# One fused transformer and state-space kernel: state-space steps by TensorE products, conditioning loads in four buffers, read-out of four rotation products

## The reference

```python
cond = jax.nn.silu(c)
for i in range(DEPTH):
    mod = cond @ ada_w[i] + ada_b[i]          # ada_w[i]: 1024 x 6144
    sh_m, sc_m, g_m, sh_f, sc_f, g_f = ...
    h = rms_norm_2(x, norm_mix[i]) * (1.0 + sc_m) + sh_m
...
def s5_mixer(h, ...):                          # 64 groups of 16 channels, 64 complex states each
    bu = einsum(u, bb)                         # complex drive of each state
    x_re, x_im = associative_scan(x[t] = ab * x[t-1] + bu[t])
    y = einsum(x_re, c_re) - einsum(x_im, c_im) + d_skip * u
    g = gelu(y);  ga, gb = split(g @ w_glu);  return ga * sigmoid(gb)
```

## Time and profile before

| what | value |
|---|---|
| median of three runs | 1781.01 us |
| profiled execution, its own time | 1783.83 us |
| its span, first to last instruction | 1782.1 us (1.7 us lie around it) |
| busy: TensorE, VectorE, ScalarE, GpSimd | 1691.1 us (95%), 797.1 (45%), 298.2 (17%), 58.8 (3%) |
| mean granted clock of TensorE | 0.975 of full speed |
| HBM read | 286.67 MB, 161 GB/s over the span |
| DMA issues | 440 weight slots and 96 conditioning blocks of 512 KB, 32 copies of H of 32 KB |

### The profile page before, as it was taken

One profiled execution on the slowest core, in us unless ns is written; L12 is line 12 of the kernel. 1 busy time (PEld: TensorE's weight loads), 2 busy tenths in 40 slices (PEclk: granted clock), 3 DMA queues, 4 the chain that ended last, 5 costly groups with the idle time before them and its releaser, 6 DMA issues.

```text
span 1782.1 us, 21562 instructions
## 1 busy us (share of the span) xinstructions
PE 1691.1 (95%) x8586; PEld 1428.3 (80%) x8586; DVE 797.1 (45%) x1732; ACT 298.2 (17%) x660; POOL 58.8 (3%) x84
## 2 busy tenths in 40 slices
PE   7989989999989999999999999999999778999998
PEld 6648878888878877888888785788888667888887
DVE  6644454341156413644345575456541274343310
ACT  2112210000024102100000322322220011122200
POOL 0000000000000000092000000000000000000000
PEclk9999999999999999999999999999999877999999
DMA  6333448865644563666554232244435302444445
GB/s 222 125 135 119 165 157 306 306 246 186 210 159 146 209 233 136 237 218 243 186 165 154 83 118 95 82 137 152 152 129 166 117 15 72 142 154 152 150 160 177
DMA packets 82900, 290.19 MB, mean 163 GB/s; under 512 B 13296, under 2 KB 13296, under 8 KB 82032
## 3 DMA queue, kind: packets, MB, share of 16 engines
q1 hardware_dynamic: 82800, 288.81, 47.8%
HBM read 286.67 MB, written 1.05 MB: 161 GB/s over the span
## 4 chain that ended last, share of the span: by engine, by line
PE 88%; DVE 8%; issue 1%; DMA 1%; ACT 1%; SPq 1%; DVEq 0%; ACTq 0%
PE acc L381 69%; PE acc L454 5%; PE acc L908 3%; PE acc L436 3%; PE acc L391 1%; PE score L582 1%; PE acc L558 1%; PE turned L593 1%; PE score L538 1%; DVE H L1383 1%; DVE rstd L1319 1%; PE acc L606 1%; SPq L348 1%; DMA ring<-stream 0%; DMA cols<-cols_in 0%
## 5 line engine op out<-in xcount | busy, mean ns | idle before, releaser
L381 PE MATMUL acc<-H,ring 128*128 128x256 f32 x3528 | 777.6, 382 | 21.7 <-DMA ring<-stream 9.9
L381 PEld LDWEIGHTS acc<-H,ring 128*128 128x128 f32 x3528 | 671.5, 191 | 126.0 <-issue 12.2
L381 PE MATMUL acc<-FFN,ring 128*128 128x256 f32 x1408 | 306.5, 381 | 0.0
L381 PEld LDWEIGHTS acc<-FFN,ring 128*128 128x128 f32 x1408 | 268.5, 191 | 37.2 <-issue 0.4
L381 PE MATMUL acc<-big,ring 128*128 128x256 f32 x880 | 192.1, 379 | 0.9 <-PE acc L381 0.9
L381 PEld LDWEIGHTS acc<-big,ring 128*128 128x128 f32 x880 | 166.9, 190 | 24.6 <-issue 2.0
L1538 DVE SCALAR_TENSOR_TENSOR bT<-bT,cond 128x1024 f32<-128x1024 f32 x84 | 109.0, 1298 | 68.1 <-DMA bT<-ada_in 61.0
L1735 DVE SCALAR_TENSOR_TENSOR pair<-acc,cols,pair 128x255 f32<-128x255 f32 x84 | 40.5, 482 | 121.5 <-ACT pair L1077 118.2
L1401 DVE TENSOR_TENSOR X<-acc,X 128x256 f32<-128x256 f32 x48 | 20.4, 425 | 156.1 <-PE acc L381 146.9
L1698 DVE TENSOR_TENSOR FFN<-pair,acc 128x256 f32<-128x256 f32 x42 | 17.7, 421 | 143.0 <-PE acc L381 142.1
L1403 DVE SCALAR_TENSOR_TENSOR X<-acc,mod,X 128x256 f32<-128x256 f32 x24 | 11.6, 484 | 147.9 <-PE acc L381 144.4
(11 more groups left out here) (407 smaller groups left out, 1327.4 us busy)
## 6 DMA issues: line engine op xcount, KB each, us to landing
ring<-stream SPq DMA_DIRECT2D x440, 512.0 KB, 3.3
bT<-ada_in SPq DMA_DIRECT2D x96, 512.0 KB, 4.4
big<-ssm_in SPq DMA_DIRECT2D x2, 1024.0 KB, 5.7
cols<-cols_in SPq DMA_DIRECT2D x1, 1169.5 KB, 7.2
X<-x_in SPq DMA_DIRECT2D x1, 1024.0 KB, 4.8
MEM<-mem_in SPq DMA_DIRECT2D x1, 1024.0 KB, 12.1
FFN<-H SPq DMA_DIRECT2D x32, 32.0 KB, 1.9
y_out<-X SPq DMA_DIRECT2D x1, 1024.0 KB, 3.9
```

What stands on the lines that cost most here:

```text
L381: mm = nc.tensor.matmul(dst, w[:, k * cols_per:(k + 1) * cols_per], r, start=first and n == 0, stop=last and n == len(src) - 1)
```

## The change

It does three things.

1. Conditioning blocks 0 to 53 go through four buffers (two in `bT`, two in `K`) in place of two; the others through the two in `bT` as before. The queue's wait before a block is on the last block that used the same buffer. In `up0` four blocks are issued after slots 0 to 3, none after 4 to 7, one after each of 8 to 31, and then eight; in `od_xb` the four blocks are issued after slots 0, 1, 6 and 7 (before: 0, 2, 4, 6), and used after tiles 2, 3, 6, 7 (before: 2, 3, 4, 5).
2. The norm of the state-space stage is one VectorE instruction a tile (into FFN), and ScalarE adds the shift and reorders the tokens (`shifted`). The copy of H is no longer made by 32 DMAs: TensorE picks the 32 channels by products with columns of the identity (`select`: 16 products with 128x32 weights and 64 columns a tile), and ScalarE copies the bank to FFN (`moved`).
3. VectorE's step has 8 instructions in place of 12: the rotation of the drive is two products of 512 columns, the two scans are one of 512 columns, and the rotation back is left as four products (one instruction of 512 columns and two of 256) whose sums `read_out` makes with twice the products (64 a tile, 128 records). `decays` fills 504 columns in place of 252; a memset gets smaller.

```diff
-    ("up0", list(range(28)) + list(range(28, 44, 2))), ("down0", range(0, 24, 4)), ("od_xb", range(0, 8, 2)),
+    ("up0", [0, 1, 2, 3] + list(range(8, 32)) + [32, 34, 36, 38, 40, 41, 42, 43]), ("down0", range(0, 24, 4)),
+    ("od_xb", (0, 1, 6, 7)),
+N_WIDE = 54
+ADA_HOME = [a % (4 if a < N_WIDE else 2) for a in range(N_ADA)]
+ADA_FREE = [max((b + 1 for b in range(a) if ADA_HOME[b] == ADA_HOME[a]), default=0) for a in range(N_ADA)]
-        ada_ring = [bT[:, i * SLOT:(i + 1) * SLOT] for i in range(2)]
+        ada_ring = [bT[:, i * SLOT:(i + 1) * SLOT] for i in range(2)] + [K[:, i * SLOT:(i + 1) * SLOT] for i in range(2)]
 # SyncE
-                    if ada >= 2:
-                        sp.wait_ge(ada_used, ada - 1)
+                    if ADA_FREE[ada]:
+                        sp.wait_ge(ada_used, ADA_FREE[ada])
-                if s == SLOT0["glu"] + RING - 1:
-                    for half in (1, 0):
-                        sp.wait_ge(norm_out, S5_NORMED + (2 if half else 4))
...
 # TensorE
+            def select(n):
+                i = S5_ORDER[n]
+                pe.wait_ge(s5_shifted, n + 1)
+                if n >= 2:
+                    pe.wait_ge(s5_moved, n - 1)
+                for jj in range(4):
+                    for j in range(CHUNK):
+                        mm = nc.tensor.matmul(turned[n % 2][32 * j:32 * j + 32, jj * CHUNKS:(jj + 1) * CHUNKS],
+                                              ident[:, 32 * jj:32 * jj + 32],
+                                              H[:, i * S + j * CHUNKS:i * S + (j + 1) * CHUNKS], start=True, stop=True)
+                mm.then_inc(s5_selected, 1)
-                    for part in range(2):
+                    for part, term in ((0, 0), (1, 1), (1, 2), (0, 3)):
-            for n in range(4):
-                local(n)
+            select(0)
+            select(1)
+            local(0)
             driven(0)
+            select(2)
             driven(1)
+            select(3)
+            local(1)
+            select(4)
+            select(5)
+            local(2)
+            select(6)
+            select(7)
+            local(3)
 # ScalarE
+            def shifted(n):
+                i = S5_ORDER[n]
+                act.wait_ge(s5_gained, n + 1)
+                nc.scalar.activation(at(H, i).rearrange("p (j c) -> p j c", j=CHUNK),
+                                     at(FFN, 16 + i).rearrange("p (c j) -> p j c", j=CHUNK), ACT.Identity,
+                                     bias=mod[:, 48 + i:48 + i + 1]).then_inc(s5_shifted, 1)
+            def moved(n):
+                i = S5_ORDER[n]
+                act.wait_ge(s5_selected, n + 1)
+                nc.scalar.activation(at(FFN, i), turned[n % 2][:, 0:S], ACT.Copy).then_inc(s5_moved, 1)
+            shifted(0)
+            for n in range(1, KD):
+                shifted(n)
+                moved(n - 1)
+            moved(KD - 1)
 # VectorE
-                if 2 <= k < 6:
+                if k in (2, 3, 6, 7):
                     ada(1)
-            scaled(X, KD, rstd[:], lambda k: mod_gain(1, 0, k), H, shift=lambda k: mod_col(1, 0, k), by_chunk=True)
+            for n, i in enumerate(S5_ORDER):
+                v.scalar_tensor_tensor(at(FFN, 16 + i), at(X, i), mod_gain(1, 0, i), rstd[:], ALU.mult, ALU.mult)\
+                    .then_inc(s5_gained, 1)
-                own(v.tensor_tensor(by_tile(a), by_tile(bank[:, :]), rot, ALU.mult))
-                own(v.tensor_tensor(b[:, re], bank[:, im], cos_i, ALU.mult))
-                own(v.tensor_tensor(b[:, im], bank[:, re], sin_i, ALU.mult))
+                own(v.tensor_tensor(by_tile(a), by_tile(bank), cos2, ALU.mult))
+                own(v.tensor_tensor(by_tile(b), by_tile(bank), sin2, ALU.mult))
                 dve.sem_inc(s5_driven, 1)
-                own(v.tensor_tensor(z[:, re], a[:, re], a[:, im], ALU.add))
-                own(v.tensor_tensor(z[:, im], b[:, re], b[:, im], ALU.subtract))
+                own(v.tensor_tensor(z[:, re], a[:, re], b[:, im], ALU.add))
+                own(v.tensor_tensor(z[:, im], a[:, im], b[:, re], ALU.subtract))
                 dve.wait_ge(s5_decays, n + 1)
-                own(v.tensor_tensor_scan(w[:, re], d, z[:, re], 0.0, ALU.mult, ALU.add))
-                own(v.tensor_tensor_scan(w[:, im], d, z[:, im], 0.0, ALU.mult, ALU.add))
-                own(v.tensor_tensor(by_tile(a), by_tile(w), rot, ALU.mult))
-                own(v.tensor_tensor(b[:, re], w[:, re], sin_i, ALU.mult))
-                own(v.tensor_tensor(b[:, im], w[:, im], cos_i, ALU.mult))
+                own(v.tensor_tensor_scan(w, d, z, 0.0, ALU.mult, ALU.add))
+                if n == 0:
+                    dve.wait_ge(s5_shifted, KD)
                 if n >= 2:
                     dve.wait_ge(s5_y, n - 1)
-                own(v.tensor_tensor(x[:, re], a[:, re], a[:, im], ALU.subtract))
-                own(v.scalar_tensor_tensor(x[:, im], b[:, re], -1.0, b[:, im], ALU.mult, ALU.subtract))
+                own(v.tensor_tensor(x[:, re], w[:, re], cos_i, ALU.mult))
+                own(v.scalar_tensor_tensor(x[:, im], w[:, im], -1.0, cos_i, ALU.mult, ALU.mult))
+                own(v.scalar_tensor_tensor(by_tile(x[:, 2 * S:4 * S]), by_tile(w), -1.0, sin2, ALU.mult, ALU.mult))
                 dve.sem_inc(s5_state, 1)
```

More of the change, by code:

```diff
@@ L66 @@
 assert N_ADA == 96 and ADA_AFTER == sorted(ADA_AFTER)
+N_WIDE = 54
+ADA_HOME = [a % (4 if a < N_WIDE else 2) for a in range(N_ADA)]
+ADA_TURN = [ADA_HOME[:a].count(ADA_HOME[a]) + 1 for a in range(N_ADA)]
+ADA_FREE = [max((b + 1 for b in range(a) if ADA_HOME[b] == ADA_HOME[a]), default=0) for a in range(N_ADA)]
 PARTS0, _n = {}, 0
@@ L242, in build_program @@
         mod_done = sem("mod_done")
-        ada_loaded = [sem(f"ada_loaded{i}") for i in range(2)]
+        ada_loaded = [sem(f"ada_loaded{i}") for i in range(4)]
         ada_used = sem("ada_used")
@@ L270, in build_program @@
         s5_kernels_out = sem("s5_kernels_out")
-        s5_moved = [sem(f"s5_moved{i}") for i in range(2)]
+        s5_gained = sem("s5_gained")
+        s5_shifted = sem("s5_shifted")
+        s5_selected = sem("s5_selected")
+        s5_moved = sem("s5_moved")
         s5_driven = sem("s5_driven")
@@ L340, in _ @@
                     sp.dma_start(V, ssm_in[1]).then_inc(c_in, 16)
-                if s == SLOT0["glu"] + RING - 1:
-                    for half in (1, 0):
-                        sp.wait_ge(norm_out, S5_NORMED + (2 if half else 4))
-                        for jj in range(4):
-                            for j in range(CHUNK):
-                                dst = FFN[32 * j:32 * j + 32, half * 1024:half * 1024 + 1024]
-                                src = H[32 * jj:32 * jj + 32, half * 1024:half * 1024 + 1024]
-                                sp.dma_start(dst.rearrange("p (i q c) -> p i q c", q=4, c=CHUNKS)[:, :, jj, :],
-                                             src.rearrange("p (i q c) -> p i q c", q=CHUNK, c=CHUNKS)[:, :, j, :])\
-                                    .then_inc(s5_moved[half], 16)
             sp.wait_ge(acc_free, 4 + TILE0["down3"] + 8)
@@ L846, in _ @@
             down("down2")
-            assert outs[0] == S5_NORMED
             sums(KD - 1)
-            outs[0] += 4
             def local(n):
                 i, t = S5_ORDER[n], TILE0["s5"] + n
-                pe.wait_ge(norm_out, S5_NORMED + 1 + n // 2)
+                pe.wait_ge(s5_shifted, n + 1)
                 bank_free(t)
@@ L887, in read_out @@
                                                   x[:, lo:lo + CHUNKS - 1], start=False,
-                                                  stop=l == CHUNK - 1 and part == 1)
+                                                  stop=l == CHUNK - 1 and term == 3)
                 mm.then_inc(s5_y, 1)
             pe.wait_ge(s5_kernels_out, 1)
-            for n in range(4):
-                local(n)
+            select(0)
+            select(1)
+            local(0)
             driven(0)
+            select(2)
             driven(1)
+            select(3)
[6 more added lines that the diff above has]
+            local(3)
             for n in range(KD):
@@ L1332, in inverse_rms, with scaled @@
                 inverse_root(out)
-            def scaled(src, tiles, factor, gain, dst, first=0, to=0, shift=None, by_chunk=False):
+            def scaled(src, tiles, factor, gain, dst, first=0, to=0, shift=None):
                 for lo in reversed(range(0, tiles, 2)):
@@ L1530, in ada @@
                     layer, cb, k = a // 48, a // 8 % 6, a % 8
-                    dve.wait_ge(ada_loaded[a % 2], 16 * (a // 2 + 1))
+                    dve.wait_ge(ada_loaded[ADA_HOME[a]], 16 * ADA_TURN[a])
+                    row = ada_ring[ADA_HOME[a]]
                     if a == 48:
@@ L1535, in ada @@
                     if k == 0:
-                        own(v.tensor_scalar(sums, ada_ring[a % 2], cond[:, k:k + 1], None, ALU.mult))
```

(11 more changed lines are left out.)

23 lines of the change are left out of this document (10 added, 13 removed).

## The result

| | before | after |
|---|---|---|
| median, us | 1780.72 (4 runs, 1780.15 to 1784.26) | 1766.26 (4 runs, 1762.15 to 1767.46) |
| profiled execution, us (span) | 1783.83 (1782.1) | 1762.15 (1760.4) |
| ratio after to before | | 0.9911, interval 0.9889 to 0.9932 |

The change makes the kernel 14.5 us faster on the medians. The forecast was 32.1 us, and 1766.3 lies above its range.

The account below looks back on a forecast made before the run. It took TensorE's own work (88% of the span) as the bound, so gains are TensorE's waits: 8.2 + 7.1 - 0.9 + 17.7 = 32.1 us off 1783.8 gives 1751.7, on the median 1748.9; range 1743 to 1760.

Parts of the forecast that it names:

- the stall at up0's start: up0: the 5.19 us wait for weight slot 3 and the half-speed stretch behind it go, 8.2 us gained.
- od_xb: od_xb: TensorE's 4.67 us stop for a weight slot and the slower records behind it go, 7.1 us gained.
- the state-space stage: State-space stage: earlier start and steps of 5.4 us in place of 6.79, less a slower last read-out, 17.7 us gained.
- (c): State-space loop: TensorE becomes the bound; 1778 at half clock, 1754 at read-outs of 3.2 us; chance 0.08.
- (e): State-space read-outs and selects: 32-column products don't overlap, slower than before, about 1802 us; chance 0.03.
- rival (a): Last state-space read-out: the clock stays up before it, 2.9 us more gained, 1746.0 us; chance 0.12.
- what it may cost is in up0: up0: conditioning blocks issued later may stop TensorE once per two pairs, six times; 0.9 us lost.
- rival (b): up0: conditioning blocks land late, in 5.7 us, 8.1 us lost, 1756 us; chance 0.10.
- this very chain: up0: from a slot's end through block issue, landing and VectorE to the freed bank, 6.8 us at a 4.3 us landing.

Follow-up runs that it names:

- e4_two_buffers: The changed kernel with its conditioning loads as before the change (two buffers, old lists in up0 and od_xb), state-space part kept: 1763.6 us.
- e1_old_slots: The changed kernel, four buffers kept, with up0's conditioning blocks issued behind the same slots as before the change: 1748.9 us.
- e11_again: The changed kernel unedited, measured a second time: 1766.6 us.
- e2_lru_first: The changed kernel with the lru parameters (small VectorE instructions) computed ahead of the wait for pair 17's block: 1762.7 us.
- e10_one_later: The changed kernel with blocks 16 to 40 of up0 each asked for one slot later: 1834.6 us.
- e6_locals_later: `e1_old_slots` with ScalarE's shifted(3) to shifted(7) ahead of moved(2), and TensorE's local(2) and local(3) behind read-outs 0 and 1: 1749.5 us.
- e9_dma_copies: `e1_old_slots` with the norm on VectorE and the 32 DMA copies of H as before the change, new steps kept: 1758.1 us.

## Why the prediction was half right

**Right: the stall at up0's start** (8.2 us forecast) is gone, with its stretch at clock 0.50: with the old list and four buffers up0 takes 145.2 us where it took 153.6, 8.4 less. **Right: od_xb** (7.1 forecast). One piece where the earlier trace rows had two with 4.67 us between:

```profile
506.79 20.96 PE L378 MATMUL acc<-H,ring 128*128 128x256 f32 x96
```

From the first to the last of these products it is 7.4 us less than before; putting the old loads back costs 6.1 us on the medians, 7.7 in the trace. Both together measured 14.6 us on the medians (`e4_two_buffers` to `e1_old_slots`) against 15.3.

**Right: the state-space stage** (17.7 us forecast). From the 1/rms to the first product of the GLU it took 75.3 us, now 56.5, and the GLU itself went from 57.56 to 55.52: 20.8 us in the profiles, 17.3 on the medians. The pieces, at the start of the loop and at its end (timelines of after):

```profile
1411.13 3.26 DVE L2063 SCALAR_TENSOR_TENSOR FFN<-X,modgain,rstd 128x256 f32<-128x256 f32 x8
1412.55 1.08 PE L865 MATMUL turned<-H,cols 128*32 128x64 f32 x32 [5.60 <-ACT H L1265]
1418.49 0.69 DVE L2078 TENSOR_TENSOR FFN<-score,chunk_tab 128x512 f32<-128x512 f32 x1 [4.11 <-PE score L879]
1420.98 1.22 DVE L2084 TENSOR_TENSOR_SCAN FFN<-probs,FFN 128x512 f32<-128x512 f32 x1
1425.53 0.43 DVE L2089 TENSOR_TENSOR FFN<-FFN,chunk_tab 128x256 f32<-128x256 f32 x1 [3.33 <-ACT H L1265]
1427.51 1.97 PE L893 MATMUL acc<-FFN,big 128*32 128x63 f32 x128
1429.41 2.00 PE L879 MATMUL score<-FFN,bT 128*128 128x64 f32 x16
...
1460.24 3.52 PE L893 MATMUL acc<-FFN,big 128*32 128x63 f32 x128 [1.60 <-DVEq L2092]
1465.74 1.97 PE L893 MATMUL acc<-FFN,big 128*32 128x63 f32 x128 [1.99 <-DVEq L2092]
```

Counted from the 1/rms, VectorE's first step was forecast at 8.3 us and came at 7.4; the wait for `shifted` behind the first scan at 3 and came at 3.33; the first read-out at 16.8 and came at 16.4; the last state at 54.7 and came at 54.6. The last two read-outs are 5.50 us apart, with 5.4 forecast for a step. The scan of 512 columns took 1.22 us (1.23). A read-out of 128 records takes 1.90 us from its start to the next one's (1427.51 to 1429.41), 15 ns a record, so rivals (c) and (e) did not come. The Trainium skill's floor of about 25 ns between starts ("TensorE: Matmul & The Clock Gate", section "Wait — 56ns, not 53.3ns?") doesn't hold for these products. The last read-out took 1.97 us: in this run the clock stayed up there, which is rival (a), for which the forecast had 20.6 us. One read-out earlier it did not (3.52). In `e11_again`, the same kernel, the last one was slow too:

```profile
1473.26 3.20 PE L893 MATMUL acc<-FFN,big 128*32 128x63 f32 x128 [3.53 <-DVEq L2092]
```

The stage with its GLU then took 118.9 us in place of 116.6. So (a) is a matter of the run, worth 2.3 us.

**The step that failed: "what it may cost is in up0".** The prediction took 0.9 us for the new list of up0; measured were 16.0 in the profile and 17.3 on the medians. Its place and rival (b), conditioning blocks land late, were right, its size was not, in three ways. The chain of a late pair, from the timelines of the SP queue, VectorE and TensorE in after:

```profile
272.82 0.33 SPq L332 DMA_DIRECT2D ring<-stream  x1
273.19 0.43 SPq L336 DMA_DIRECT2D bT<-ada_in  x1
...
277.86 1.29 DVE L1573 SCALAR_TENSOR_TENSOR bT<-bT,cond 128x1024 f32<-128x1024 f32 x1 [2.20 <-DMA bT<-ada_in]
279.40 0.42 DVE L1733 TENSOR_TENSOR FFN<-pair,acc 128x256 f32<-128x256 f32 x1 [0.25 <-DVE bT L1573]
279.97 14.05 PE L378 MATMUL acc<-H,ring 128*128 128x256 f32 x64 [0.27 <-DVE FFN L1733]
```

From the ring's issue to TensorE are 7.15 us, of which 4.67 are from the block's issue to its use; TensorE wants the bank after 6.9. The prediction had written this very chain and got 6.8. The chain was right to 0.1 us: with 6.8 us at a landing of 4.3 it leaves 4.4 for the landing, which is what the single waits show. First, the *landing*: its median was 4.6 us in this run and 5.0 to 5.3 in `e11_again`, not the 4.3 of the earlier trace rows, and single blocks took up to 6.4 us here and up to 7.5 in `e2_lru_first`. The prediction put one excess of 0.15 us into all six waits; the seven small waits have a mean of 0.7 us, in `e11_again` 1.1. Their number was about right. With a slack of 0.1 us in 6.9, a term of 0.9 was a bet on the lowest row and on no spread. The waits from it are 4.7 us in the one run and 7.8 in the other; in `e2_lru_first` they are 9.6 in up0.

Second, *the lru parameters*, which the prediction didn't see. In pair 17 they stand on VectorE between the block and the product:

```profile
379.84 0.43 SPq L336 DMA_DIRECT2D big<-ada_in  x1
...
384.41 1.28 DVE L1573 SCALAR_TENSOR_TENSOR bT<-big,cond,bT 128x1024 f32<-128x1024 f32 x1 [4.85 <-DMA big<-ada_in]
...
395.48 0.42 DVE L1733 TENSOR_TENSOR FFN<-pair,acc 128x256 f32<-128x256 f32 x1 [0.25 <-DVE softp L1711]
```

Between 385.8 and 395.2 lie nothing but instructions of 0.17 to 0.20 us. Before, the block was at hand and these ran while TensorE worked on the pair; now they start only when the block has landed, and TensorE waits 6.25 us. No sentence of the prediction asked what else is queued behind the late block on VectorE.

Third, *the clock*: the prediction counted the price of lower clock at the stalls that go, not at the waits that come. Behind 6.25 us of idle time the clock is 0.61 for 8 us (stretch, its us, busy by engine, clock):

```profile
396.00:404.00 8.00, 7.95 (x23) 6.52 (x24) 2.99 (x3) 0.38 (x1) 0.00 (x0) 0.61 0.03 6
404.00:420.00 16.00, 16.00 (x76) 13.81 (x75) 3.41 (x4) 0.77 (x2) 0.00 (x0) 1.00 0.72 261
```

That is 24.02 - 20.96 = 3.1 us. The sum in the profiled run: 4.7 small waits, 6.25 the long one, 3.1 for the clock, 14.1 of the 16.0 us; the other 2 are the ends of nine pieces, 0.2 us each: 64 records take 14.05 us as a piece and 13.84 within the 672 of `e1_old_slots`. Without its term of 0.9 the forecast would have been 1748.0, and with up0's list undone (`e1_old_slots`) the kernel takes 1748.9: the other terms were right in sum, and this one is all of the miss. What stays open is why the stage's 20.8 us in the profiles are 17.3 on the medians, so that these don't decide between the forecast's 17.7 and its 20.6 for (a).

## What to carry to other kernels

A load that is asked for when the consumer passes a point has a slack of (time to its need) less (issue, landing, use, semaphores). When that comes within the spread of the landing time, as 0.1 us in 6.9 here, cost it by the slow landings and not by the typical one. Then ask whether the next request goes out before the wait or behind it: before it, every second round was stopped here, behind it every round. List everything that stands behind the late item on each engine, the rare blocks of work as well: 9.4 us of small instructions were free while the item was early and cost 6 us once it was late. To every new wait of some us on TensorE add the work at the lower clock behind it: it cost half again the longest wait here, and nearly as much again as the wait in `e10_one_later`.

## What the runs showed of the hardware

Idle time that recurs cost nearly twice its length: 3.5 us idle every pair, and 32 records in 10.18 us in place of 7.14, a mean clock of 0.76 over 100 us. An idle time of 0.3 to 2 us between pieces of 14 us left the records at full size in up0 (64 in 14.05 us behind 2.04 us idle). In the state-space loop, though, 1.60 us were followed by a read-out of 3.52 us in place of 1.97, and 1.99 us by one at full size.

Blocks of 512 KB that go out beside a weight slot every 3.45 us landed in 4.6 to 5.3 us at the median, differently in two executions of one kernel, whose small waits differed by 3.1 us. Single blocks took up to 7.5 us (in `e2_lru_first`).

Pauses of TensorE marked "issue" (2.02 us in `e6_locals_later`, 2.17 in after, 0.67 in `e9_dma_copies`) ended 2.3 to 2.7 us behind the start of a transfer of the kind "instruction". That the one causes the other is not shown.
